# Encoder layer: the steps of a triangular inverse spread over the slots of the gate weights by element count, ending at slot 49 of 64

## What is computed

```python
proj = u @ w_in[i]
rw_seg, q, k, v, gate_a, gate_b = jnp.split(proj, col_split, axis=-1)
y_a = rwkv7_branch(...)            # two recurrences over 256 positions, 16 heads each
y_b = diff_attention_branch(...)
merged = sigmoid(gate_a) * (y_a @ w_branch_a) + sigmoid(gate_b) * (y_b @ w_branch_b)
h = h + rms_norm(merged @ w_out, mix_post_g)
```

## Time and profile before

| | |
|---|---|
| median of 3 runs | 2553.21 us (2552.71 to 2554.07) |
| the profiled execution | 2548.16 us |
| its span, first to last instruction | 2546.4 us |
| TensorE busy | 94% of the span |
| VectorE busy | 56% |
| ScalarE busy | 42% |
| stage of the gates and the wait behind it | about 1114 to 1343 us of the span |
| granted TensorE clock, mean | 0.969 of full speed |

### The profile page before, as it was taken

One profiled execution on the slowest core, in us unless ns is written; L12 is line 12 of the kernel. 1 busy time (PEld: TensorE's weight loads), 2 busy tenths in 40 slices (PEclk: granted clock), 3 DMA queues, 4 the chain that ended last, 5 costly groups with the idle time before them and its releaser, 6 DMA issues.

```text
span 2546.4 us, 31751 instructions
## 1 busy us (share of the span) xinstructions
PE 2390.2 (94%) x12010; PEld 1943.1 (76%) x12010; DVE 1413.5 (56%) x1672; ACT 1060.4 (42%) x1393; POOL 127.8 (5%) x177
## 2 busy tenths in 40 slices
PE   7999999999989999998788977789899999999997
PEld 5888888888878777786567845678688888888885
DVE  4555544445555558979954454555554454455454
ACT  5444434444446645543232224434544443444442
POOL 0000000000000012210001030000000000000000
PEclk9999999999999999999898978899999999999998
DMA  6666556666557555675481033366566656666653
GB/s 227 190 188 190 189 192 195 191 185 192 191 156 226 174 167 181 194 250 160 142 237 52 9 95 99 102 221 191 159 188 190 190 188 194 194 190 189 190 183 131
DMA packets 225605, 443.79 MB, mean 174 GB/s; under 512 B 22574, under 2 KB 24796, under 8 KB 223836
## 3 DMA queue, kind: packets, MB, share of 16 engines
q1 hardware_dynamic: 206720, 397.72, 51.5%
q0 software_dynamic: 9488, 39.76, 4.7%
q10 hardware_dynamic: 9292, 4.87, 0.7%
HBM read 423.42 MB, written 18.87 MB: 174 GB/s over the span
## 4 chain that ended last, share of the span: by engine, by line
PE 84%; DVE 11%; DMA 2%; ACT 2%; issue 1%; POOL 0%; SPq 0%; DVEq 0%; ACTq 0%; POOLq 0%
PE ps L1306 25%; PE ps L1308 25%; PE ps L1307 25%; DVE wlo L809 3%; DVE z L1062 2%; DVE zt L1057 2%; DMA raw<-in_w_in 1%; PE ps L1344 1%; PE ps L1535 1%; PE ps L1494 1%; PE ps L1520 1%; PE ps L1327 1%; PE ps L1510 1%; PE ps L1536 1%; DVE h L866 1%
## 5 line engine op out<-in xcount | busy, mean ns | idle before, releaser
L809 DVE TENSOR_TENSOR wlo<-raw,whi 128x1024 fp32r<-128x1024 f32 (+1 forms) x760 | 930.4, 1228 | 916.1 <-ACT whi L464 913.9
L464 ACT ACTIVATE whi<-raw 128x1024 fp32r<-128x1024 f32 (+1 forms) x760 | 801.8, 1058 | 1113.8 <-PE ps L1308 1026.7
L1306 PE MATMUL ps<-whi,uhi 128*128 128x512 f32 (+1 forms) x2208 | 873.9, 396 | 30.1 <-DVE wlo L809 29.9
L1307 PE MATMUL ps<-wlo,uhi 128*128 128x512 f32 (+1 forms) x2208 | 863.6, 391 | 0.0
L1308 PE MATMUL ps<-whi,ulo 128*128 128x512 f32 (+1 forms) x2208 | 863.3, 391 | 0.0
L1306 PEld LDWEIGHTS ps<-whi,uhi 128*128 128x128 f32 x2208 | 417.6, 189 | 131.0 <-DVE wlo L809 38.6
L1308 PEld LDWEIGHTS ps<-whi,ulo 128*128 128x128 f32 x2208 | 417.5, 189 | 87.2
L1307 PEld LDWEIGHTS ps<-wlo,uhi 128*128 128x128 f32 x2208 | 418.0, 189 | 83.0
L1306 PE MATMUL ps<-whi,hthi 128*128 128x512 f32 x704 | 274.2, 389 | 0.0
L1308 PE MATMUL ps<-whi,htlo 128*128 128x512 f32 x704 | 273.9, 389 | 0.0
L1307 PE MATMUL ps<-wlo,hthi 128*128 128x512 f32 x704 | 273.9, 389 | 0.0
(11 more groups left out here) (260 smaller groups left out, 1489.0 us busy)
## 6 DMA issues: line engine op xcount, KB each, us to landing
raw<-in_ffn_w_gu SPq DMA_DIRECT2D x352, 512.0 KB, 3.6
raw<-in_ffn_w_down SPq DMA_DIRECT2D x176, 512.0 KB, 3.7
raw<-in_w_in SPq DMA_DIRECT2D x160, 512.0 KB, 3.7
raw<-in_w_out SPq DMA_DIRECT2D x32, 512.0 KB, 4.2
raw<-in_w_branch_a SPq DMA_DIRECT2D x16, 512.0 KB, 4.3
raw<-in_w_branch_b SPq DMA_DIRECT2D x16, 512.0 KB, 3.8
gate_dram<-gst_g POOLq DMA_DIRECT2D x8, 512.0 KB, 4.6
gbuf<-gate_dram POOLq DMA_DIRECT2D x8, 512.0 KB, 4.2
```

Of the source, the lines that this page charges most:

```text
L464: nc.scalar.activation(whi[:, s, :, 0:p.width], raw[:, s, :, 0:p.width], ACT.Copy).then_inc(hi_ready, 1)
L809: V.tensor_tensor(wlo[:, s, :, 0:p.width], raw[:, s, :, 0:p.width], whi[:, s, :, 0:p.width].bitcast(F32), ALU.subtract).then_inc(lo_ready, 1)
L1306: mm(o, at, w_, start=(j == 0 and k == 0), stop=False)
L1307: mm(o, at, l_, start=False, stop=False)
```

## The change

`steps_before` changes, and nothing else. A step gets the weight 160 + s x (63 - s), so a constant for its two operations plus its elements; the 63 weights sum to 51744. The steps are handed out so that the sum of the weights grows in a straight line, from slot 8 to slot 50 instead of 55. As the lists come out:

| slot | steps before | steps after |
|---|---|---|
| 8 | 0 | 0 to 4 |
| 9 | 1 | 5 to 7 |
| 10 | 2, 3 | 8, 9 |
| 16 | 10, 11 | 18 |
| 24 | 21 | 27 |
| 31 | 30, 31 | 35 |
| 40 | 42, 43 | 45 |
| 48 | 53 | 57, 58, 59 |
| 49 | 54, 55 | 60, 61, 62 |
| 50 to 53 | 56; 57; 58, 59; 60 | none |
| 54 | 61, 62 | none |

From slot 16 to slot 41 there is one step a slot, but for slots 19, 30 and 38, which have two.

```diff
--- before.py
+++ after.py
@@ -1039,10 +1039,13 @@
 
             ones = z[:, :, :].rearrange("p c t -> p (c t)")[:, 0:C * C:C + 1]
 
+            STEP_WORK = [160 + s * (C - 1 - s) for s in range(C - 1)]
+
             def steps_before(k):
 
-                first, last = 8, slots - 9
-                return min(max(k - first, 0) * (C - 1) // (last - first), C - 1)
+                first, last = 8, slots - 14
+                share = min(max(k - first, 0) / (last - first), 1)
+                return next(i for i in range(C) if sum(STEP_WORK[:i]) >= share * sum(STEP_WORK) - 1)
 
             def step(s):
                 if s == 0:
```

## The result

The changed kernel takes **2558.63 us** in the median of its runs (2556.60 to 2560.53), the kernel before, run beside it on the same chip, 2551.45 (2546.14 to 2554.07). The difference of the medians is 7.2 us; the ratio, which compares the means of the runs and not their medians, is **1.0032, with a 95% interval from 1.0022 to 1.0041**: slower, and the interval is well clear of 1. The profiled execution took 2559.35 us, its span is 2557.6.

A forecast was written before the change was run, and what follows sets the result against it. VectorE paces the middle of the gate stage; the inverse's load starves the end of weights. Slot 58 ready at 1324.2, plus 5.05 and 13.6, ends at 1342.8, not 1335.2: +7.6 on 2553.21, 2560.8; range 2549.5 to half a us above 2564.1.

The forecast's parts named there:

- The end of the inverse: VectorE, saturated in the gate stage, finishes the inverse 5.9 us earlier, at 1292.5, with five fewer splits ahead of it.
- TensorE at slot 50: In the gate stage, TensorE is 5.6 us later at slot 50, which ends at 1296.5 instead of 1290.9.
- the gap: TensorE's idle time near the end of the gates, waiting for held-back weights: 6.61 us before, 8.7 forecast.
- The store and loads: On GpSimd's queue, the inverse's store at 1292.8 and loads at 1302.3; the gate store queued behind costs 0.
- The weight queue: Slot 54's weights 0 to 1.0 us late; slot 58's held back, ready at 1324.2, so TensorE idles 8.7 us.
- The rest: Slot 58 at the lower clock, 5.05 us, then slots 59 to 63, 13.6: end at 1342.8, +7.6 us.
- The hand-over: From the end of the gates to the recurrence's start: ScalarE's output, four splits and VectorE's preparation, 8.0 us, unchanged.
- two slots passing (B): Weights of slots 58 and 59 pass, four slots are left after slot 60 is ready: about +1 us; chance 0.15.
- equal shares (F): Two DMA queues share the slow stretch equally, slots 59 to 61 each 2.3 to 2.8 us late: +4.5 us; chance 0.06.
- the gap that closes (C): Loaded slots 54 to 57 and quicker weights cover the slow stretch, TensorE never idles there: -3.3 us; chance 0.11.
- Clock loss by even starving (D): TensorE idling 1 us in every 3.75 lowers its clock, two slow slots add 4.7: +12.3 us; chance 0.10.

The follow-up runs named there:

- pair with wide loads: Inverse loaded by two DMAs of all 128 partitions and half the columns each: changed kernel 2551.94 us, ratio 1.0006; kernel before 2544.99 us, ratio 0.9980.
- handout by count: Kernel before, its steps handed out by count as there, but ending at slot 49 instead of 54: 2560.86 us, ratio 1.0034.
- long rows: Inverse loaded in rows of 4096 numbers instead of 64: changed kernel 2557.93 us, ratio 1.0028; kernel before 2553.53 us, ratio 1.0011.
- run with two queues: Changed kernel ending at slot 57, one half of the inverse loaded from SyncE's queue beside GpSimd's: 2544.22 us, ratio 0.9975.

## Why the prediction was right, point by point

It said +7.6 us, at 2560.8, and the medians gave +7.2, at 2558.63. The forecast started from a median of three runs, 1.8 us above the one of eleven, and that makes most of the distance between the two times. By its own steps:

1. **The end of the inverse.** Forecast 1292.5, 5.9 us earlier; it is 1293.02 + 0.28 = 1293.3, and counted from the matrices' landing 157.6 us, where it was 163.2: 5.7 earlier. VectorE had no idle time until then. Right.
2. **TensorE at slot 50.** Forecast 5.6 us later; found 6.1, counted from the landing of the matrices. The pair with wide loads measures it without the gap: 7.2 us, of which 0.86 is the wait at slot 54. The forecast's sum does not contain this term, though. It counts from the landing of slot 58, and TensorE's lateness is swallowed by the gap ahead of it. The ends at slots 44 (with the store of gates moved) and 54 give 1.67 and 1.59 us a slot, against 5.6 / 5 = 1.1 here, or 1.54 as a slot less a split.
3. **The store and loads.** Forecast 1292.8 and 1302.3; found 1293.60 and 1301.78. The store of gates queued behind cost nothing. What the step did not see is the one ahead: it was issued at 1290.06, 3.5 us before the inverse was ready. It was out of the way by luck of a few us; with the handout by count, or with the end at slot 44, it is not. The working looked only behind the moved DMAs on GpSimd's queue.
4. **The weight queue.** Slot 54 was forecast 0 to 1.0 us late and was in time. Slot 58 was forecast to be the one held back, landed at 1321.7 and ready at 1324.2: ScalarE begins it at 1322.03 after 13.12 us, and TensorE at 1324.40. The gap was forecast at 8.7 us and is 7.65, because TensorE came to it later (1316.75 for 1315.5). That error costs nothing, since the end of the gap hangs on the DMAs and not on TensorE.
5. **The rest.** Six slots in 18.65 us from 1324.2 gave 1342.8; measured 1342.71 - 1324.40 = 18.3, ending at 1342.7. In it slot 58, forecast at the 5.05 us of slot 63 before, took 4.5. The hand-over took 8.01 us. Recurrence forecast at 1350.8, found at 1350.68, or 1350.15 counted from the landing of the matrices. This is the 0.65 us between +7.6 and the stage's +6.95: slot 58 ready 0.3 us sooner, its slow run 0.55 shorter, the five slots behind it 0.2 longer.

As for the rivals, two slots passing (B) and equal shares (F) fall with slot 58's wait of 13.12 us, and the gap that closes (C) with the 7.65. Clock loss by even starving (D) falls with the clock of 0.96 from 1215 to 1255, and with the 9 of 39 us that TensorE idled from 1136 at a clock of 1.00. The gain in clock brought nothing either, as the forecast had it: VectorE sets the pace in that stretch.

**What the working had wrong** is a cause, not a term. It said that "the rate halves while the load moves its rows of 64 numbers". The long rows took the rate from 182 to 205 GB/s only; all 128 partitions took it to 404. The forecast survived because the change leaves the loads as they are. The Trainium skill, "SBUF — State Buffer", section "Door 1: The DMA port swizzle", has this rule: partitions 0 to 63 reach only half of the 16 ports, and a 1 MB transfer to them was measured there at 196 GB/s beside 328 for all 128. The runs agree, with 205 to 211 beside 388 to 404. The Trainium skill, same page, section "Can I just issue two DMAs to hit both halves?", has two transfers to the two halves at only 6% above one. The run with two queues agrees in that the full rate did not come back, at 165 GB/s with short rows; a gain of 6% it is too coarse to show.

And the working never asked what the earlier end is for. It followed the gap and saw that it stays; it did not say that the gap costs both kernels nearly the same, nor that the better place for the end is later. At slot 57 the same handout is 13.9 us faster than at slot 49, and about 7 faster than the kernel before. Not run, and open: wide loads in the right order (the store would have to lay out the inverse for them) with the end at slot 57.

## What to carry to other kernels

Where a helper engine is saturated by side work that it does between the feeds of the main engine, an earlier due time for the side work makes the main engine wait beside it; put its end later, up to what its reader allows, and find that place by trying both directions (of the ends tried here, 44, 49, 54 and 57, the last was the best, and none later was run). An even handout was worth nothing here, where the sum of the work set the pace. A large load to half of the partitions nearly closed the queue beside it: give such a load all 128. And ask of everything moved on an in-order queue what stands ahead of it as well as behind.

## What the runs showed of the hardware that was not expected

- A load from memory to 64 partitions halves what all queues of the core move together: 205 to 211 GB/s with rows of 4096 numbers, against 388 to 404 for the same bytes to 128 partitions, with the 16 DMA engines busy 96% and more in both. With rows of 64 numbers it is 182 to 191 over 15 us, and 165 over 11 us with both halves in flight from two queues.
- Beside such a load the other queue does not get half. In the changed kernel 182 GB/s over 15 us are 2.7 MB: an estimate from that leaves, beside the 2.1 MB of the load, little more than one slot of weights (0.5 MB). Four slots issued into it took 16.3 us in the median, where 3.6 is usual.
- How much TensorE idles does not tell its clock. In the changed kernel it idled 9 of the 39 us from 1136 to 1175, in gaps of 0.2 to 2.1 us, at a granted clock of 1.00. From 1215 to 1255 it idled about as much, in gaps of about 0.5 us, one of 3.0 and, at the end, one of 2.5, and the clock fell to the lower level for some 4 us behind each of these two (the second time behind the stretch, which shows 0.96). In the kernel before the same stretch has three gaps of 2.8 to 3.0 us, each with such a fall, and 0.87. Nor does the length of the last gap alone tell it: the clock fell after a gap of 1.8 us (changed kernel, 1269), and it stayed at 1.00 after one of 2.3 (kernel before, 1257) and one of 3.0 (the run with two queues, 1141). What decides was not tested.
